# A decoder layer with retrieved experts on one Trainium2 core: the normalised row in two banks of PSUM, attention scores of both components in one score bank in turn, and the loop of tile 0 begun with a quarter of its choice

## The reference, cut to what matters

```python
def hybrid_layer(x, ...):
    z = rmsnorm(x, norm1_g) @ w_in                 # q | k | v | pooling branch
    ...                                            # QK-norm, rotary
    att = diff_attn(q, k_all, v_all, ...)          # 4 heads, 2 components each
    ...
    x = x + concat([att, pool_y]) @ w_out
    x = x + peer(rmsnorm(x, norm2_g), w_query, sub_keys, w_u, w_v)

def diff_attn(q, k, v, q_pos, k_pos, lam):
    p = softmax(mask(einsum('bqhcd,bkhcd->bchqk', q, k) * 64 ** -0.5))
    a = p[:, 0] - lam * p[:, 1]
    return einsum('bhqk,bkhd->bqhd', a, v)

def peer(x, w_query, sub_keys, w_u, w_v):          # 8 heads, 128 x 128 experts
    q = (x @ w_query).reshape(T, 8, 2, 128)
    s = einsum('thcd,hcnd->thcn', q, sub_keys)     # scores of two halves of a key
    sv, si = top_k(s, 16)                          # the 16 best of each half
    cand = sv[:, :, 0, :, None] + sv[:, :, 1, None, :]
    top, sel = top_k(cand, 16)                     # the 16 best of 256 sums
    eidx = take_along_axis(cidx, sel)              # 8 x 16 = 128 experts of a row
    gate = softmax(top)
    a = gelu(einsum('td,thkd->thk', x, w_u[eidx])) * gate
    return einsum('thk,thkd->td', a, w_v[eidx])
```

## Time and profile before

| what | value |
|---|---|
| median of 3 runs | 3609.66 us (3595.9 to 3618.48) |
| the profiled execution | 3600.91 us |
| its span in the trace | 3598.9 us |
| end of the last fold | 361.2 us |
| first dot of tile 0 | 541.4 us |
| first dots of tiles 1 to 8 | 889.2, 1239.7, 1589.8, 1946.0, 2302.8, 2665.9, 3035.8, 3427.0 us |
| last dot | 3589.6 us |
| data moved | 1216 MB, 338 GB/s over the span |

### The profile page before, as it was taken

One profiled execution on the slowest core, in us unless ns is written; L12 is line 12 of the kernel. 1 busy time (PEld: TensorE's weight loads), 2 busy tenths in 40 slices (PEclk: granted clock), 3 DMA queues, 4 the chain that ended last, 5 costly groups with the idle time before them and its releaser, 6 DMA issues.

```text
span 3598.9 us, 32093 instructions
## 1 busy us (share of the span) xinstructions
PE 3062.0 (85%) x7658; PEld 1317.5 (37%) x7658; DVE 2194.4 (61%) x5098; ACT 1421.2 (39%) x3898; POOL 2340.0 (65%) x2195
## 2 busy tenths in 40 slices
PE   7999777897889789978897999788979897889877
PEld 3446453342334233323332433243324342343311
DVE  2224455588558755975497549754975487446944
ACT  1221105433643454345434543454345433543333
POOL 0000007777777777777777777777776777567776
PEclk9999879999999999999999999999999999999999
DMA  5224229999999999999999999999999999899999
GB/s 200 82 88 176 62 82 375 407 373 392 385 402 376 390 391 395 382 390 366 389 385 394 369 384 382 382 350 377 390 389 338 371 380 387 277 336 377 384 392 371
DMA packets 342466, 1216.25 MB, mean 338 GB/s; under 512 B 39641, under 2 KB 40025, under 8 KB 342153
## 3 DMA queue, kind: packets, MB, share of 16 engines
q0 software_dynamic: 313344, 1140.99, 82.8%
q1 hardware_dynamic: 28944, 73.30, 5.8%
HBM read 1200.28 MB, written 14.04 MB: 337 GB/s over the span
## 4 chain that ended last, share of the span: by engine, by line
POOL 33%; PE 29%; DVE 15%; issue 12%; ACT 7%; DMA 4%; DVEq 0%; ACTq 0%; SPq 0%; POOLq 0%; PEldq 0%
POOL big L548 13%; POOL big L541 13%; PE Y L823 12%; DVE big L1416 5%; POOL slot L541 3%; PE Y L581 3%; POOL slot L548 3%; PE S L581 3%; PE S L757 2%; DMA slot<-in_wv,idx_c 2%; DVE qpw L1252 2%; ACT L987 2%; PE S L649 2%; PE Y L739 1%; DVE qpw L1249 1%
## 5 line engine op out<-in xcount | busy, mean ns | idle before, releaser
L823 PE MATMUL Y<-big,diag 128*128 128x512 f32 (+1 forms) x3540 | 1759.7, 625 | 387.7 <-ACT diag L1003 258.6
L1416 DVE CUSTOM_DVE_ANT_0 big<-big,h2c 128x1024 f32<-128x1024 f32 x885 | 1081.2, 1229 | 603.8 <-DMA big<-in_wu,idx_c 574.0
L541 POOL DMA_INDIRECT big<-in_wu,idx_c x885 | 926.9, 1047 | 583.1 <-issue 266.0
L823 PEld LDWEIGHTS Y<-big,diag 128*128 128x128 f32 (+1 forms) x3540 | 633.4, 191 | 1381.4 <-issue 949.5
L548 POOL DMA_INDIRECT big<-in_wv,idx_c x885 | 948.0, 1071 | 274.0 <-issue 264.4
L987 ACT ACTIVATE gel<-dots 128x1 f32<-128x1 f32 x1088 | 219.2, 201 | 1295.4 <-DVE dots L1416 1243.0
L823 PE MATMUL Y<-slot,diag 128*128 128x512 f32 (+1 forms) x812 | 403.5, 620 | 70.1 <-ACT diag L1003 42.2
L1003 ACT ACTIVATE diag<-ident,amp 128x128 f32<-128x128 f32 x1024 | 411.2, 402 | 33.9
L999 ACT ACTIVATE amp<-gel,gate_c 128x1 f32<-128x1 f32 x1088 | 320.6, 295 | 130.5 <-ACT gel L987 3.6
L1416 DVE CUSTOM_DVE_ANT_0 slot<-slot,h2c 128x1024 f32<-128x1024 f32 x203 | 249.5, 1229 | 161.5 <-DMA slot<-in_wu,idx_c 154.6
L777 PE MATMUL S<-big,work 128*128 128x512 f32 x576 | 293.9, 598 | 0.8 <-issue 0.8
(11 more groups left out here) (181 smaller groups left out, 2113.6 us busy)
## 6 DMA issues: line engine op xcount, KB each, us to landing
big<-in_wu,idx_c POOLq DMA_INDIRECT x885, 6.3
big<-in_wv,idx_c POOLq DMA_INDIRECT x885, 6.4
big<-in_w_in SPq DMA_DIRECT2D x8, 1024.0 KB, 11.3
big<-in_wqT SPq DMA_DIRECT2D x4, 2048.0 KB, 7.6
big<-in_xT SPq DMA_DIRECT2D x9, 512.0 KB, 3.8
big<-in_x SPq DMA_DIRECT2D x9, 512.0 KB, 4.6
big<-in_mt SPq DMA_DIRECT2D x9, 512.0 KB, 5.2
qp_dram<-big SPq DMA_DIRECT2D x9, 512.0 KB
```

The source lines that it names most:

```text
L541: pool.indirect_dma_start(ring[s][:, 0:D], None, wu, bass.IndirectOffsetOnAxis(ap=idx_c[:, k:k + 1], axis=0)).then_inc(u_landed[s], 16)
L823: mm = pe.matmul(Y[0:w, m * 512:(m + 1) * 512], diag[:, s * P:s * P + w], ring[s][:, D + m * 512:D + (m + 1) * 512], start=(k == 0), stop= ...
L1416: dot = dve.tensor_tensor_reduce(out=ring[s][:, 0:D], in0=ring[s][:, 0:D], in1=h2c[:, :], scale=1.0, scalar=0.0, op0=ALU.mult, op1=ALU.add ...
```

## The change

The names stand as in the code after.

- `H`, the normalised row, takes the place of `h2c` in the dot and lies in the two PSUM banks that were `S1`. The dot reads one operand from PSUM and one from the ring.
- The scores of both components use `S0` in turn, component 1 first. PE may write those of component 0 only when DVE has scaled those of component 1 (`s_free`, released after each scaling). The offsets in a head become 0, 1, 3, 4 for the scores, 2 and 5 for the scaling, 3 and 6 for the exponentials. `a_used` is waited for by component 0 alone.
- Route scores have two banks instead of four; the third and fourth group wait until ACT has taken the first and second (`route_free`).
- Each tile has a table of its own (`PLAN`). Tiles 2 to 8 keep their steps except for those above. Tile 0's is compressed, so that the sample attention lies beside tile 0's attention and projection and is over before the route scores end. Tile 1's attention begins at step 33 of tile 0's loop, with 4 steps for a head.
- Only the first quarter of tile 0's choice stands ahead of the loop. The other three (30 units) go into steps 1 to 30 of its loop, one unit a step, and their indices and gates are handed over by quarters.
- `w_out` and the ring change places in one large buffer; `w_out` is loaded on ACT's queue after the last fold, the sample cache after the eighth fold instead of the sixteenth.
- `sample_values` has 16 products a sequence instead of 24: those with the new keys are made once, at the last sequence, for all.

The diff, cut to its core:

```diff
+def plan_of(t):
+    first = Plan(head0=0, headw=4, scores=(0, 0, 0, 0), scale=(0, 0), exp=(0, 0), combine=(2, 2), flip=(2, 2, 2),
+                 evac=(2, 2, 2), values=(3, 3, 3, 3), tops=40)
...
+    return first if t == 0 else second if t == 1 else Plan()
...
-        S = [S0, S1]
+        H = S1
...
-        route_bank = [S0[:, 0:512], S0[:, 512:1024], S1[:, 0:512], S1[:, 512:1024]]
+        route_bank = [S0[:, 0:512], S0[:, 512:1024]]
...
-                if u == 0:
+                if m == 0 and (turn == 0 or t > 0):
                     pe.wait_ge(s_free, n(s_free))
...
-                    for i in range(PAGES + 1):
+                    for i in range(PAGES):
...
-                if c == 1:
+                if c == 0 or t > 0:
                     dve.sem_inc(s_free, 1)
...
-                dve.scalar_tensor_tensor(h2c[:, :], x1n, r2, g2w[:, :], ALU.mult, ALU.mult).then_inc(dve_own, 1)
+                dve.scalar_tensor_tensor(H[:, :], x1n, r2, g2w[:, :], ALU.mult, ALU.mult).then_inc(dve_own, 1)
...
-                dot = dve.tensor_tensor_reduce(out=ring[s][:, 0:D], in0=ring[s][:, 0:D], in1=h2c[:, :],
+                dot = dve.tensor_tensor_reduce(out=ring[s][:, 0:D], in0=H[:, :], in1=ring[s][:, 0:D],
...
+                    if t == 0 and 1 <= k <= 3 * TOPU:
+                        q, u = divmod(TOPU + k - 1, TOPU)
+                        top_part(q, u)
+                        if u == TOPU - 1:
+                            quarter_in(q, idx_hi if q == 2 else idx_mid)
```

More of the change, by code:

```diff
@@ L94 @@
 class Plan:
[L97 to L113, removed]
-    residual, x1n_free = 16, 24
[L116 to L124, removed]
+    residual, x1n_free = 16, 24
+    def __init__(self, head0=1, headw=9, scores=(0, 1, 3, 4), scale=(2, 5), exp=(3, 6), combine=(8, 9),
+                 flip=(10, 11, 12), evac=(11, 12, 12), values=(12, 13, 14, 15), tops=44):
+        self.head0, self.headw, self.scores, self.scale, self.exp = head0, headw, scores, scale, exp
+        self.combine, self.flip, self.evac, self.values = combine, flip, evac, values
+        self.exp_last = (6, 6)
+        self.att = head0 + (HEADS - 1) * headw + values[-1] + 1
+        self.squares, self.norm, self.flip_att = self.att + 1, self.att + 3, self.att + 4
+        self.project = self.flip_att + 1
+        self.x1 = self.project + 2 * DC
+        self.flip_x1 = (self.x1 + 1, self.x1 + 2)
+        self.r2 = self.x1 + 2
+        self.route = self.x1 + 3
+        self.take = tuple(self.route + q * DC for q in range(1, 5))
+        self.top, self.tops = self.take[0] + 1, tops
+        self.gate = self.top + tops
+        self.promote = self.gate + 1
+        self.sample0, self.samplew = 0, 20
+        self.sample_out = self.sample0 + self.samplew * SEQS // GRP
@@ new lines, in head, with choice @@
+    def head(self, k, at, h):
+        return [i for i, a in enumerate(at) if k == self.head0 + self.headw * h + a]
+    def choice(self, k):
+        return [divmod(i, TOPU) for i in range(4 * TOPU) if k == self.top + i * self.tops // (4 * TOPU)]
+def plan_of(t):
+    first = Plan(head0=0, headw=4, scores=(0, 0, 0, 0), scale=(0, 0), exp=(0, 0), combine=(2, 2), flip=(2, 2, 2),
+                 evac=(2, 2, 2), values=(3, 3, 3, 3), tops=40)
+    second = Plan(head0=33, headw=4, scores=(0, 0, 2, 2), scale=(1, 3), exp=(2, 3), combine=(4, 4), flip=(5, 5, 5),
+                  evac=(5, 5, 5), values=(6, 6, 6, 6), tops=40)
+    return first if t == 0 else second if t == 1 else Plan()
@@ L127 @@
+PLAN = [plan_of(t) for t in range(TILES)]
 class Counter:
@@ L654, in scores_of @@
                     pe.wait_ge(t_free, n(t_free))
-                    for c in range(2):
+                    for c in (1, 0):
                         r = slice(QK * c, QK * c + QK)
```

194 lines of the change are left out of this document (123 added, 71 removed).

## The result

The changed kernel takes 3643.12 us (median of 4 runs, 3640.47 to 3647.66) against 3602.86 us (4 runs of the kernel before, 3595.9 to 3618.48). The ratio is 1.0107, with a 95% interval from 1.0076 to 1.0137: slower by about 1%, where 3464 us had been forecast. The profiled execution after has a span of 3645.8 us, 46.9 more than before.

What follows compares the result with a forecast made beforehand. POOL's gathers, hindered by the dot's SBUF operands, set the pace, with the DMA limit just below. 3600.9 - 73.5 (dot) - 30 (scores) - 46 (prologue) + 9 (tile 0) = 3460.4, plus 4: 3464 us; range 3390 to 3555.

Steps and rivals of the forecast that it cites:

- The scores in turn: Attention, tiles 1 to 7: waits between PE's scores and DVE's scaling hidden where PE has room; -30 us, bounds -80 and +160.
- five slots hold four steps in stock, 10 us: Gather ring in attention: stock said to cover the new score waits, so their cost from below is 0.
- The slower rival: Attention, tiles 1 to 7: score waits stop DVE twice a head, 7 us each over 28 heads, +196; total 3690; chance 0.08.
- the other terms: Forecast gains outside the slower rival's score waits, put at 141 us, which 5 us a head would eat.
- The dot: Loop of tiles 1 to 7: one PSUM operand stops hindering POOL's gathers; -10.5 us a tile, -73.5 together.
- projection and route scores: Part of the dot's term: this 40-step stretch falls from 105.5 to 102.8 us, -2.7 a tile.
- The turn: Part of the dot's term: 10 steps between tiles fall from 25.8 to 20.0 us through a full ring, -5.8 a tile.
- the choice: Part of the dot's term: 44 DVE-bound steps of 124.8 us gain little, -2 a tile, bounds 0 and -9.
- The floor of 333 us a tile: Tile's least time at the DMA limit: 128 steps at 2.56 us plus 5 us of other traffic.
- The prologue: Ahead of the loop: route scores start at 460, first dot at 495 instead of 541.4; -46 us, bounds 475 and 520.
- Tile 0 was to lose 9 us: Tile 0's loop, taking in three quarters of its choice: 357 against 347.8 us, +9, bounds -5 and +25.
- Steps 31 to 84 at 2.56 are 138: Tile 0's loop between its own choice and tile 1's: steps run at the DMA limit, 138 us.

Runs made afterwards that it cites:

- e1: The changed kernel with the normalised row back in SBUF, so the dot has two SBUF operands again: 3704.2 us, ratio 1.0283.
- e5: Row back in SBUF, against the changed kernel with scaling three steps behind scores in tiles 4 to 7 (3532.75 us): 3587.67 us.
- e6: Against that same three-step kernel (3532.75 us): two choice quarters ahead of tile 0's loop, tile 1's attention from step 22, 6 steps a head: 3513.82 us.

## Why the prediction was wrong

**The scores in turn: the step that failed.** It took the new waits "as hidden where PE has room", for -30 us, because "five slots hold four steps in stock, 10 us". Attention in tiles 1 to 7 came out 87 us longer: the stretches of tiles 1 and 2 4 us shorter each, those of tiles 3 to 6 17 to 26 longer, tile 7's 7 longer. Two things were overlooked. The stock was counted as if all slots held landed rows, but a gather lands 6.6 us after its issue (median of the page after), more than two steps of 2.56, so that over half of five slots are in flight. (That this is why the stock did not cover the stops is argued; no run changes the number of slots.) And the price of a wait was bounded by L1142's waits for ACT, 2.9 us, up to 6.9, although the same table showed the right neighbour, four waits for PE of 35.1 us in tile 8's heads, 8.8 each. The prediction says that no such hop is in the trace; it was there, with 23.0 us in 19 waits, at two or three steps' distance. In tile 5's stretch the eight waits are 61.6 us, 7.7 each. The order showed the missing steps plainly; their price was set too low. The slower rival named this mechanism, with 5 us a head as the point from which it decides. By its own sum that point is 4: without the 30 us of attention the other terms are 110.5 us, over 28 heads. It was given 0.08; in tile 5 it cost 22 us in four heads, 5.5 each. Tiles 1 and 2, with short heads, paid nothing (the waits in tile 1's stretch are 5.2 us in all), and tile 7 paid 7 us. So attention lost 87 us, not the rival's 196, and the whole stayed below its 3690.

**The dot: right in kind, given back in part.** Gathers became 0.95 us, as forecast, and undoing the operand costs 61 us (e1) or 55 (e5) against the 73.5 of the sum. But it was put in the wrong stretches. From the change to e1, on average over tiles 1 to 7, projection and route scores go from 104.6 to 110.9 us, so the operand is worth 6.3 us there, where 2.7 had been put. The turn goes from 25.2 to 27.6, 2.4 us where 5.8 had been put, and the choice from 125.7 to 124.3: there the operand costs 1.4 us, where 2 had been put as a gain. Tile 1's choice is 124.60 us (124.80 before) and its turn 26.00 (25.80). The timeline of DVE at that turn shows why there is no stock to spend:

```profile
1207.57 1.23 DVE L1463 CUSTOM_DVE_ANT_0 big<-S,big 128x1024 f32<-128x1024 f32 x1 [0.19 <-DVE gate_n L1427]
...
1208.71 1.22 DVE L1463 CUSTOM_DVE_ANT_0 big<-S,big 128x1024 f32<-128x1024 f32 x1
...
1209.86 1.22 DVE L1463 CUSTOM_DVE_ANT_0 big<-S,big 128x1024 f32<-128x1024 f32 x1
...
1216.45 1.23 DVE L1463 CUSTOM_DVE_ANT_0 slot<-S,slot 128x1024 f32<-128x1024 f32 x1 [5.36 <-DMA slot<-in_wu,idx_c]
...
1220.08 0.20 DVE L1449 COPY idx_c<-idx_n 128x64 int32<-128x64 int32 x1 [2.40 <-DMA slot<-in_wv,idx_c]
```

Three dots run back to back, and then DVE waits 5.36 and 2.40 us: the slots that they free are filled a landing later. What DVE gains by running through a full ring it waits for again behind it. The floor of 333 us a tile held all stretches at the DMA limit; with the choice on DVE at 125 us the rest of a tile, 84 steps at 2.56 and 5 us of other traffic, makes 345, which is what tile 2 takes (345.3).

**The prologue: better than forecast, but given back.** First dot at 482.2, not 495:

```profile
451.18 27.70 PE L793 MATMUL S<-big,work 128*128 128x512 f32 x64 [0.85 <-issue]
```

Route scores start at 451.2 (460) and take 27.7 us (32.5). Tile 0 was to lose 9 us and lost 42.6. Its first 31 steps, choice and dots together, took 93.2 us, as worked out (93), and the 40 steps of tile 1's choice 120.5 (119). The term that failed is "Steps 31 to 84 at 2.56 are 138": it costed tile 1's attention, moved into 20 steps, at nothing. These steps took 165.3 us; steps 37 to 64 among them took 92.40 where they had taken 68.8 before the change, and e6 shows that room for the attention gives the time back.

**The sum.** Prologue -59, tile 0 +43, attention of tiles 1 to 7 +87, their other stretches -20, tile 8 -4: +47, the difference of the spans. The forecast had -46, +9, -30, -73.5 and 0.

## What to carry to other kernels

Where two engines hand work back and forth inside a loop, count the steps between producer and consumer in each engine's own order, and compare them with the distance that the producer already runs behind: a consumer that stands closer stops, and everything queued behind it with it. A ring's depth is a stock only for what has landed; the part in flight, latency over step time (here 6.6 us over 2.56), has to be taken off first. And a change that is slower as a whole can hold a part that is worth keeping: undo its parts one by one before it is dropped, and look at the offsets before the idea.

## What the runs showed that was not expected

DVE has a cost of its own when POOL is freed. The conversion of 128x32 numbers behind a unit of choice, before (L1316) and after (L1361); duration min, median and max in ns:

```profile
L1316 DVE CAST idx_n<-maskw x36: 180/181/182, 443.1 to 3405.1; 128x32 int32<-128x32 f32 x36
```

```profile
L1361 DVE CAST idx_n<-maskw x36: 181/420/425, 476.2 to 3455.8; 128x32 int32<-128x32 f32 x36
```

Its median goes from 181 to 420 ns, and in e5, with the row in SBUF again, it is 181. The trace says when: after the change 33 of the 36 conversions begin while a gather is under way on POOL, some 0.5 us after its start, and they end with it; the other three, with no gather under way at their start, take 181 or 182 ns. Before the change all 36 begin with no gather under way. The Trainium skill, "SBUF — State Buffer", section "Who interferes with whom", says that a cast can, when its operands meet certain conditions, take the port pair that DVE shares with GpSimd, and that the one that comes second waits. The trace agrees: 420 ns for those that come second. Four of them in a tile are about 1 us, half of the 2.0 us by which the choice of tiles 1 to 7 is longer on average than before the change (125.7 against 123.7).
